# The last pair's expert rows reach their tokens by a matrix product instead of a trip through HBM

## The reference, cut to what matters

```python
g_w, g_idx = lax.top_k(softmax(tok @ w_rg + b_rg), 1)              # one of 4 groups
e_w, e_idx = lax.top_k(softmax(e_sel), TOP_K)                      # 2 of its 8 experts
weights = g_w * e_w / sum(e_w)                                     # two gates for each token
xs = tok[order // TOP_K]                                           # 512 rows sorted by expert
ys = ragged_dot(silu(ragged_dot(xs, w_gate)) * ragged_dot(xs, w_up), w_down)
out = einsum('nkd,nk->nd', ys[inv].reshape(N, TOP_K, D), weights)  # back to tokens
x = x + ga2 * rmsnorm(out, ln2_post)
```

## Time and profile before

| what | us |
|---|---|
| median of 3 runs | 1236.36 (1234.91 to 1242.99) |
| the profiled execution | 1236.75, its span 1235.0 |
| DMA moving 418 GB/s, all 16 engines busy | 1000 to 1192 of the span |
| last weight piece waited for (gate of pair 15) lands | 1192.1 |
| last matmul record of pair 15's down product ends | 1211.7 |
| Y of pair 15 in SBUF | 1212.5 |
| its rows in `spread` | 1215.9 |
| first token block back in SBUF | 1220.8 |
| end of the span | 1235.0 |

### The profile page before, as it was taken

One profiled execution on the slowest core, in us unless ns is written; L12 is line 12 of the kernel. 1 busy time (PEld: TensorE's weight loads), 2 busy tenths in 40 slices (PEclk: granted clock), 3 DMA queues, 4 the chain that ended last, 5 costly groups with the idle time before them and its releaser, 6 DMA issues.

```text
span 1235.0 us, 20589 instructions
## 1 busy us (share of the span) xinstructions
PE 1149.7 (93%) x8444; PEld 971.9 (79%) x8444; DVE 663.8 (54%) x1217; ACT 524.8 (42%) x916; POOL 103.0 (8%) x165
## 2 busy tenths in 40 slices
PE   6999999999999999989999999799987789989993
PEld 4888888999999887879999999778886545545551
DVE  4555557888744655457789754666455431111103
ACT  5444445555643444444565644464553221111112
POOL 5000000000000000000040000000000011212210
PEclk9999989999999899989999999899997899999997
DMA  9444346777546345245776556334335399999982
GB/s 292 128 166 154 128 127 203 208 222 212 173 166 191 115 135 170 85 154 171 213 225 177 182 172 193 103 103 116 90 129 247 117 387 418 417 418 417 416 333 108
DMA packets 199513, 252.67 MB, mean 205 GB/s; under 512 B 19808, under 2 KB 179084, under 8 KB 187132
## 3 DMA queue, kind: packets, MB, share of 16 engines
q1 hardware_dynamic: 185312, 223.55, 53.1%
q0 software_dynamic: 13744, 27.67, 6.5%
q10 hardware_dynamic: 363, 0.14, 0.0%
HBM read 273.34 MB, written 11.53 MB: 231 GB/s over the span
## 4 chain that ended last, share of the span: by engine, by line
PE 73%; DMA 11%; DVE 7%; ACT 4%; issue 3%; SPq 1%; DVEq 0%; ACTq 0%; POOLq 0%
PE ps L775 17%; PE ps L776 16%; PE ps L777 16%; DMA wy<-in_w_exp_gate 9%; PE ps L2512 4%; PE ps L2525 3%; PE ps L717 2%; ACT whi L747 2%; PE ps L2115 2%; DMA raw<-in_w_exp_gate 1%; DVE wlo L756 1%; PE ps L2182 1%; PE ps L2116 1%; PE ps L2504 1%; PE ps L2153 1%
## 5 line engine op out<-in xcount | busy, mean ns | idle before, releaser
L775 PE MATMUL ps<-xhi,whi 128*128 128x272 f32 (+2 forms) x1424 | 430.1, 302 | 19.7 <-DVE xlo L771 10.9
L776 PE MATMUL ps<-xlo,whi 128*128 128x272 f32 (+2 forms) x1424 | 414.0, 291 | 0.0
L777 PE MATMUL ps<-xhi,wlo 128*128 128x272 f32 (+2 forms) x1424 | 412.4, 290 | 0.0
L756 DVE TENSOR_TENSOR wlo<-raw,whi 128x2048 fp32r<-128x2048 f32 (+1 forms) x115 | 259.4, 2255 | 159.6 <-ACT whi L747 159.5
L775 PEld LDWEIGHTS ps<-xhi,whi 128*128 128x128 f32 x1424 | 275.2, 193 | 34.2 <-issue 25.0
L747 ACT ACTIVATE whi<-raw 128x2048 fp32r<-128x2048 f32 (+1 forms) x115 | 216.2, 1881 | 149.8 <-PE ps L777 149.7
L776 PEld LDWEIGHTS ps<-xlo,whi 128*128 128x128 f32 x1424 | 275.2, 193 | 0.9 <-issue 0.5
L777 PEld LDWEIGHTS ps<-xhi,wlo 128*128 128x128 f32 x1424 | 274.7, 193 | 0.0
L775 PE MATMUL ps<-hhi,whi 128*128 128x272 f32 (+1 forms) x352 | 100.7, 286 | 0.7 <-DVE wlo L756 0.6
L776 PE MATMUL ps<-hlo,whi 128*128 128x272 f32 (+1 forms) x352 | 100.2, 285 | 0.0
L777 PE MATMUL ps<-hhi,wlo 128*128 128x272 f32 (+1 forms) x352 | 99.9, 284 | 0.0
(11 more groups left out here) (420 smaller groups left out, 1569.9 us busy)
## 6 DMA issues: line engine op xcount, KB each, us to landing
raw<-in_w_up SPq DMA_DIRECT2D x88, 512.0 KB
raw<-in_w_in SPq DMA_DIRECT2D x33, 1024.0 KB
ada<-in_w_ada POOLq DMA_DIRECT2D x48, 512.0 KB, 5.1
raw<-in_w_exp_gate SPq DMA_DIRECT2D x16, 1024.0 KB
raw<-in_w_exp_up SPq DMA_DIRECT2D x16, 1024.0 KB
wx<-in_w_exp_down SPq DMA_DIRECT2D x16, 1024.0 KB
wy<-in_w_exp_gate SPq DMA_DIRECT2D x16, 1024.0 KB
raw<-in_w_down SPq DMA_DIRECT2D x16, 896.0 KB
```

The lines of the kernel that those rows point to most:

```text
L756: dve.tensor_tensor(wlo[SLOT[n]][:, 0:nk, :], raw[n % RAW][:, 0:nk, :], whi[SLOT[n]][:, 0:nk, :].bitcast(F32), ALU.subtract).then_inc(s_w_ ...
L775: pe.matmul(dst, ah, bh, start=first, stop=False, **kw)
L776: pe.matmul(dst, ah, bl, start=False, stop=False, **kw)
L777: return pe.matmul(dst, al, bh, start=False, stop=last, **kw)
```

## The change

1. `PHASE_FROM` is 3: every overflow phase moves one pair earlier, none is left at p = 15.
2. POOL fills `Yb[:, 1]` with zeros at the start of the stage and scatters them to the last pair's rows of `spread`. The last pair's Y is no longer scattered; SP loads `spread` when the 19 others (and the zeros) are there.
3. `last_rows` (128 slots x 256 tokens) holds in column `n` the gate of token `n` in the slot where the last pair has its row, else 0. DVE builds it at p = 0 (compare) and p = 2 (times the gates, which PE spreads over the partitions). At the end four products `last_rows` x `Yb` give the last pair's share in PSUM, and DVE adds them (`tail_z`).
4. The residual is transposed by PE at p = 15 and copied to `Xtok`; the gain is spread by PE at p = 15 and copied to `gain`; the gates are computed at p = 1; the table of log and exp is loaded ahead of the last `y_left`.
5. The last `y_left` waits for the left half of the down product alone (event `half`).
6. The tail becomes: add (`tail_z`), times gain (`tail_g`), times root plus residual (`done`), each in four pieces of 512 columns.

```diff
-PHASE_FROM = 4
+PHASE_FROM = 3
+RESID_BANK = [(0, 3), (6, 7)]
+LAST_BANK = [(1, 2), (0, 3)]
...
-            sp.wait_ge(s_scat[0], 16 * ((len(Y_ORDER) + 1) // 2))
+            sp.wait_ge(s_scat[0], 16 * (len(Y_ORDER) // 2))
...
-            for p in range(NPAIR + 1):
+            fill(Yb[:, 1, :], 0.0)
+            pool.indirect_dma_start(out=spread[:, :], out_offset=bass.IndirectOffsetOnAxis(ap=dest[:, NPAIR - 1:NPAIR], axis=0),
+                                    in_=Yb[:, 1, :], in_offset=None, bounds_check=SLOTS - 1,
+                                    oob_is_err=False).then_inc(s_scat[1], 16)
+            for p in range(NPAIR):
...
-                act.wait_ge(s_w_used.sem, s_w_used.after(("dn", 0, ab[1]), 0))
+                if ab == PAIRS[-1]:
+                    act.wait_ge(s_resid.sem, s_resid.after("half"))
+                else:
+                    act.wait_ge(s_w_used.sem, s_w_used.after(("dn", 0, ab[1]), 0))
...
+                if p == NPAIR:
+                    act.wait_ge(s_gain.sem, s_gain.after(0))
+                    act.activation(gain[:, 0:512], ps[0][:, :], ACT.Copy).then_inc(s_tail_act.sem, s_tail_act.event("gain"))
+                    act.preload_act_table_set("natural_log_exp_and_others")
                 if p >= 1:
                     y_left(PAIRS[p - 1])
+                if p == NPAIR - 1:
+                    for t in range(2):
+                        act.wait_ge(s_resid.sem, s_resid.after(t, 0))
+                        act.activation(Xtok[:, t, 0:512], ps[RESID_BANK[t][0]][:, :], ACT.Copy).then_inc(s_tail_act.sem, s_tail_act.event("resid", t))
...
+                if p == NPAIR:
+                    sum_rows(0)
                 if p >= 1:
                     y_right(PAIRS[p - 1])
...
+                    r(dve.tensor_scalar(last_rows[:, :], iota[:, :], 1.0, inv[:, NPAIR - 1:NPAIR], ALU.add, ALU.is_equal))
                     overflow()
+                if p == 1:
+                    gates()
+                if p == 2:
+                    dve.wait_ge(s_moe_sums.sem, s_moe_sums.after("gates"))
+                    r(dve.tensor_tensor(last_rows[:, :], last_rows[:, :], ps[3][:, :], ALU.mult))
+                    dve.tensor_tensor(last_rows[:, 0:T2], last_rows[:, 0:T2], last_rows[:, T2:2 * T2], ALU.add).then_inc(s_tail_dve.sem, s_tail_dve.event("last_rows"))
...
+            sum_rows(1)
...
+                    dve.tensor_tensor(yl[:, t, 1, cs], ps[LAST_BANK[t][h]][:, :], yl[:, t, 1, cs], ALU.add).then_inc(s_tail_dve.sem, s_tail_dve.event("tail_z", t, h))
...
+                    dve.tensor_tensor(yl[:, t, 0, cs], yl[:, t, 1, cs], gain[:, cs], ALU.mult).then_inc(s_tail_dve.sem, s_tail_dve.event("tail_g", t, h))
...
+                    dve.scalar_tensor_tensor(yl[:, t, 1, cs], yl[:, t, 0, cs], ss[:, t:t + 1], Xtok[:, t, cs], ALU.mult, ALU.add).then_inc(s_tail_dve.sem, s_tail_dve.event("done", t, h))
...
             for h in range(2):
+                if h == 0:
+                    pe.wait_ge(s_y_left.sem, s_y_left.after(len(Y_ORDER) - 1))
+                else:
+                    pe.wait_ge(s_y_right.sem, s_y_right.after(len(Y_ORDER) - 1))
+                for t in range(2):
+                    pe.matmul(ps[LAST_BANK[t][h]][:, :], last_rows[:, P * t:P * t + P], Yb[:, 1, 512 * h:512 * h + 512],
+                              start=True, stop=True).then_inc(s_resid.sem, s_resid.event("last", t, h))
```

More of the change, by code:

```diff
@@ L224, in build @@
         sq = sb("sq", [P, 4, T])
+        rs_at = top[0]
         rs = sb("rs", [P, 2, T])
@@ L342, in build @@
         Yb = over_tile("Yb", (XN_at, 4 * KT * T), [P, 2, D])
+        last_rows = over_tile("last_rows", (rs_at, 8 * T), [P, SLOTS])
+        Xtok = over_tile("Xtok", (xlo_at, 4 * KT * T), [P, 2, D])
+        gain = over_tile("gain", (wo0_at, 4 * 8 * CW), [P, D])
+        junk = over_tile("junk", (sq_at, 16 * T), [P, D])
         iota = over_tile("iota", (slope_at, 2 * ATT_H * P), [P, SLOTS])
@@ L2040, in _ @@
                 f, q, kind = phase_at(p)
+                if p == NPAIR:
+                    sum_rows(0)
                 if p >= 1:
                     y_right(PAIRS[p - 1])
+                if p == NPAIR - 1:
+                    for t in range(2):
+                        dve.wait_ge(s_resid.sem, s_resid.after(t, 1))
+                        dve.tensor_copy(Xtok[:, t, 512:1024], ps[RESID_BANK[t][1]][:, :]).then_inc(s_tail_dve.sem, s_tail_dve.event("resid", t))
                 if p < NPAIR:
@@ L2527, in halves_narrow @@
                                            start=(j == 0), stop=(j == 1))
+                            if h == 0 and j == 1 and half_ == 1 and ab == PAIRS[-1]:
+                                mm.then_inc(s_resid.sem, s_resid.event("half"))
                             if h == 1 and j == 1:
@@ L2578, in phase @@
             def phase(f, q, kind):
+                if f == 0:
+                    pe.wait_ge(s_tail_dve.sem, s_tail_dve.after("last_rows"))
                 if kind == "ga":
@@ L2619, in _ @@
                     narrow(p - 1)
+                if p == NPAIR - 1:
+                    y_banks_free(Y_ORDER.index(PAIRS[p]))
+                    for t in range(2):
+                        for h in range(2):
+                            for j in range(4):
+                                o = pe.transpose(ps[RESID_BANK[t][h]][:, P * j:P * j + P], XT[:, 4 * h + j, META + P * t:META + P * t + P], ident[:, :])
+                            o.then_inc(s_resid.sem, s_resid.event(t, h))
                 if p < NPAIR:
@@ L2623, in _ @@
                     phase(f, q, kind)
[L2624 to L2630, removed]
-            for h in range(2):
-                for j in range(4):
-                    k = 4 * h + j
-                    o = pe.matmul(ps[4 + h][:, P * j:P * j + P], gsc[:, 3, k:k + 1].broadcast_to([P, P]), ident[:, :], start=True, stop=True)
-                o.then_inc(s_gain.sem, s_gain.event(h))
+                if p == 2:
+                    pe.wait_ge(s_tail_dve.sem, s_tail_dve.after("gates"))
+                    for j in range(2):
+                        for t in range(2):
+                            c = T2 * j + P * t
+                            o = pe.matmul(ps[3][:, c:c + P], rt[:, t, 107 + j:108 + j].broadcast_to([P, P]), ident[:, :], start=True, stop=True)
+                    o.then_inc(s_moe_sums.sem, s_moe_sums.event("gates"))
@@ new lines, in _ @@
+                if p == NPAIR - 1:
+                    pe.wait_ge(s_tail_act.sem, s_tail_act.after("resid", 0))
+                    pe.wait_ge(s_tail_dve.sem, s_tail_dve.after("resid", 0))
+                    for h in range(2):
+                        for j in range(4):
+                            k = 4 * h + j
+                            o = pe.matmul(ps[3 * h][:, P * j:P * j + P], gsc[:, 3, k:k + 1].broadcast_to([P, P]), ident[:, :], start=True, stop=True)
+                        o.then_inc(s_gain.sem, s_gain.event(h))
+                    pe.wait_ge(s_tail_act.sem, s_tail_act.after("resid", 1))
+                    pe.wait_ge(s_tail_dve.sem, s_tail_dve.after("resid", 1))
```

47 lines of the change are left out of this document (29 added, 18 removed).

## The result

| kernel | median, us | runs |
|---|---|---|
| before | 1237.63 (1234.91 to 1242.99) | 16 |
| changed | 1226.82 (1224.75 to 1236.12) | 16 |

The ratio is 0.9917, with a 95% interval of 0.9901 to 0.9933: 0.83% faster, clear of no change, and short of 1%. The forecast was 1226.5, worked out from the 1236.36 us of the first three runs of the kernel before; with 16 runs its median is 1237.63. The profiled execution took 1228.51 us, its span is 1226.8 against 1235.0.

A forecast was written before the change was run, and what follows sets the result against it. Weight bytes bound the kernel to 1192, then PE and a 23.3 us serial tail. DVE's end at 1222.2 plus 2.5 and 0.4 reserve gave span 1225.1, 9.9 less than 1235.0, hence 1226.5 us; range 1222.3 to 1233.5.

The forecast's parts named there:

- Step 1: PE from 1192 on: overflow product 3.5 us out, residual transposes and gain 3.6 in; pair 15's down product ends at 1211.6.
- Step 2: Overflow phase at p = 3 and stream start: delay of at most 0.74 us hidden under the full weight queue; costs nothing.
- Step 3: SP's early load of `spread`: blocks land at 1209.3 and 1211.3, 1.2 and 0.3 us before ACT wants them.
- reserve of 0.4: 0.4 us added to the span's end for hand-offs between engines that may not fit margins of 0.3 to 0.7 us.
- Step 4: ACT in the tail: table load to 1209.8, `y_left` to 1210.5, two scalings to 1211.6 and 1212.8.
- Rival (e): ACT's table load holds its queue for twice 1.28 us, `y_left` and all behind 1.3 us later: 1227.8; chance 0.02.
- Step 5: DVE's queue sets the tail's end: no gap from the first sum at 1211.7 to the last operation's end at 1222.2.
- The sum: Span's end: 1222.2 + 2.5 + 0.4 reserve = 1225.1, 9.9 us less than 1235.0, hence a median of 1226.5.
- (a): Larger gain: PE's stretch at p = 15 shortens as well and the reserve isn't needed; 1222 to 1224; chance 0.18.
- (b): Load of `spread` comes late, delaying ACT's scaling, DVE's sum and PE's last products; 1229 to 1231; chance 0.12.
- (c): PE's clock falls to 1.2 GHz with the 16 transposes ahead of `widen("gb", 15)`; 13 us more, 1239.4; chance 0.04.
- (d): Weight stream starves at its start: pair 1's down product delayed over 4 us or queue drained; 1228 to 1250; chance 0.03.

The follow-up runs named there:

- x_phase: The kernel before with the overflow phases one pair earlier (PHASE_FROM 3) and nothing else; 1236.56 us, ratio 0.9977.
- x_phase4: The changed kernel with phases at p = 4 to 15 again, the last ahead of the residual and `widen("gb", 15)`; 1238.84 us, ratio 1.0009.
- y_order: The changed kernel with gain spread at p = 2, pair 14's down product ahead of `widen("ga", 15)`, half the residual behind `widen("gb", 15)`; 1228.82 us, ratio 0.9917.
- z_after: The changed kernel, unchanged, timed again beside z_full (y_order plus ACT copying Y's right half and DVE adding block by block); 1228.11 us, ratio 0.9912.
- x_free14: The changed kernel with pair 14's rows also sent as zeros at the stage's start, their share missing from the result; 1228.39 us, ratio 0.9904.
- y_after: The changed kernel, unchanged, timed again on the same chip as y_order; 1228.76 us, ratio 0.9932.

## Why the prediction was right

The last gate product of the profiled execution stands 1.34 us later than in the one before (1193.55 against 1192.21); predicted times below are moved by that.

- **Step 1, PE.** Predicted end of the down product 1211.6 + 1.34 = 1212.94; PE's last record of it ends at 1213.09. From the last gate product to that end it took 19.47 us before and 19.54 now. "3.5 out, 3.6 in" holds, but x_phase shows that the 3.5 were worth 2.6 alone. The sum came out because the gain's product stands where the phase had stood, and in part that was luck. I had this as a matter of PE's records only; what they cover on ACT and DVE belongs to it.
- **Step 2, start of the stream.** The hole near 990 is the same: by the windows view 264 GB/s in 990 to 995 before, 261 now. SP's issue of the down piece behind pair 1's down product came 25.25 us behind the first issue (1003.67 - 978.42), 24.30 before (1001.75 - 977.45): 0.95 us later and not at most 0.74. That was hidden as forecast: with a second fill it came at 25.91 in z_fill2, and the last gate product no later. "Nothing" for the stream as a whole may be 0.4 us too little: from the first issue to the last gate product it took 214.76 us before and 214.70 in x_phase4, but more in all eight profiles with the phases from p = 3 (y_order and its like, which change PE's order ahead of that product, left aside): 214.91 in z_fill2, 215.13 in the changed kernel, 215.18 in x_phase, up to 215.76 in z_after (where PE had waited 0.93 us for the indirect load of the last phase) and 216.27 in x_free14. x_phase changes nothing else, so the phase is the likely cause. It is not shown: three profiles of the same changed kernel differ by 0.6 us among themselves (215.13, 215.22, 215.76), and how the phase would delay the last piece was not tried.
- **Step 3, spread read early.** Scatter start to SP's load 2.6 us, as predicted. The landing of the slowest block was taken from one row, 6.8 us; it was 7.5 in the first profile, 6.7 in both repeats and 6.8 in z_fill2. The margin of 0.3 us held in none of the three profiles of the changed kernel: ACT waited for the second block 1.29 us in the first profile and 0.44 us in the repeats. DVE lost 0.55 us by it in the first profile, more than the reserve of 0.4 that had been meant for it, and nothing in the repeats, since the copy of Y's right half stands between its two sums. y_after:

```profile
1212.14 1.15 ACT L1446 ACTIVATE yl<-yl,rt 128x1024 f32<-128x1024 f32 x1 [0.44 <-DMA yl<-spread]
...
1213.54 1.27 DVE L2041 SCALAR_TENSOR_TENSOR yl<-yl,rt 128x1024 f32<-128x1024 f32 x1
```

- **Step 4, ACT.** The table load ends at 1211.17, predicted 1211.14, and the copy of Y's left half starts at 1211.42 after 0.25 us of waiting for PE. Rival (e) did not happen. The Trainium skill (ScalarE: Activation LUTs, What ACT_TABLE_LOAD costs) would have the queue held for 2.66 us in all, to 1212.55; here it was free 1.28 us behind the load's start, and the load had begun 0.02 us behind the end of the copy ahead of it (1209.28 + 0.59), so the trace disagrees.
- **Step 5, DVE.** First sum predicted at 1213.04, measured 1213.09. The three groups of four took 2.47, 2.48 and 2.73 us; predicted from the earlier trace rows were 2.48, 2.48 and 2.72. This is where the forecast's accuracy came from: durations of the same shape, and the step within a queue taken from rows of two.
- **The sum.** Predicted tail 32.9 (42.8 less 9.9), of which 0.4 was reserve, measured 33.25, and 32.6 in both repeats. The median came 0.3 us above the forecast. That it came so close is partly luck: the forecast was worked out from 1236.36 us, and against the 1237.63 of 16 runs the gain is 10.8 us, not 9.9. The better test of the mechanism is the tail, 9.5 to 10.2 us shorter.
- **The rivals.** (a) did not happen: its reserve of 0.4 was not needed in the repeats, but PE's stretch did not shorten, and a tail 2.5 us or more under the forecast was not seen. (b) happened to the extent of 0.6 us in the first profile, and its chain in full in x_phase4. (c): the clock stayed at 1.00 through both groups of 16 records and up to 1218, so this rival is out. The Trainium skill (TensorE: Matmul & The Clock Gate, Part 4: PE-mode transpose) says that a transpose doesn't count as PE being busy in the same way; between the long products of this place that made no difference. (d): no starvation, at most the 0.4 us above.

## What to carry to other kernels

The last tile of a scatter through HBM can be kept on the chip: what it costs is one small product with a table built under the memory-bound part. What it saves is most of the trip: 8.7 us here against the same code with the trip, 7.0 against the best code with the trip. The two differ because work that a trip would cover costs time when it is put ahead of the last product: move it there only together with taking the trip out. The rest must then be ready early, and every producer ahead of the last tile counts: with one overflow product left ahead of pair 15's up product the same code gained nothing. When a filler product is taken out of a queue, ask which latency of the other engines it had covered, and put other work in its place.

## What the runs showed of the hardware that was not expected

**A fill by POOL holds VectorE's short instructions.** The changed kernel at the start of the stage:

```profile
986.12 1.23 POOL L908 MEMSET Yb<- 128x1024 f32 x1 [84.25 <-DVE dest L1914]
986.49 0.89 DVE L2047 TENSOR_SCALAR over<-offn 128x32 f32<-128x32 f32 x1
...
986.84 0.63 DVE L2048 TENSOR_SCALAR val_o<-iota 128x32 f32<-128x32 f32 x1
987.37 0.16 DVE L2049 TENSOR_SCALAR val_o<-offn 128x32 f32<-128x32 f32 x1
```

Five of them take 0.63 to 0.89 us where the next ones, alone, take 0.17, and all end at about 987.4, with the fill. In the kernel before, without a fill, all nine take 0.17. With two fills, in z_fill2:

```profile
986.30 2.24 POOL L908 MEMSET Yb<- 128x1024 f32 x2 [84.24 <-DVE dest L1915]
986.67 0.89 DVE L2048 TENSOR_SCALAR over<-offn 128x32 f32<-128x32 f32 x1
...
987.54 1.03 DVE L2050 TENSOR_SCALAR val_o<-offn 128x32 f32<-128x32 f32 x1
...
987.79 0.84 DVE L2050 TENSOR_SCALAR val_o<-offn 128x32 f32<-128x32 f32 x1
```

four more are held, to 988.6, the end of the second fill. So it is the fill that holds them (one profile of each kernel). The last short one ends 0.65 us later against the first issue (988.63 - 978.61 = 10.02, against 987.79 - 978.42 = 9.37), less than the 1.0 to 1.5 us I expected. No cost to the kernel is seen: z_fill2's stage, 247.5 us, is not longer than the changed kernel's.

**An indirect scatter of the same 128 rows took 2.6 us with DMA nearly idle (41 and 0 GB/s) and 4.8 us against the last 172 GB/s of a stream**, from POOL's start to SP's next issue. In x_free14 the last scatter before the load, 128 rows of an overflow pair, stood against 336 GB/s and took 7.1 us, from this row to SP's issue at 1206.87:

```profile
1199.73 0.99 POOL L1017 DMA_INDIRECT spread<-Yb,dest  x1 [6.89 <-DVE Yb L2043]
```

That the stream is the cause fits all of these and was not isolated.

**Indirect loads were waited for by PE** for 0.80, 0.77 and 1.25 us at 1034.55, 1050.15 and 1065.98 of the changed kernel and for 2.45 us in x_phase4, while the weight queue was full or just drained. I had treated these loads as free.
